# Row sums of the modulation sections by another route, a reciprocal root in two parts, and two moved steps on ScalarE

## The chip, the core and the metric

The kernel runs on one core of a Trainium2 chip. Its engines work side by side, each through its own queue in order: TensorE (PE, matrix products and transposes; the loading of its stationary operand is shown apart as PEld), VectorE (DVE), ScalarE (ACT), GpSimd (POOL, nearly unused here), and SyncE (SP), which issues the weight transfers. They meet through semaphores. The metric is the device time of one execution in microseconds (us), the median of the runs shown. Lower is better.

## What is computed

Two transformer stacks of two layers each, one after the other, on 256 tokens of width 1024 (batch 1, all float32). In the first stack the six vectors that modulate each layer (shift, scale and gate, for the mixer and for the feed-forward part) come from a conditioning vector `c` through a 1024 x 6144 matrix, so that there are twelve sections of 1024 numbers. Cut to what the change touches:

```
for i in range(DEPTH):                                  # 2 layers: differential attention, short convolution
    mod = (silu_c @ ada_w[i] + ada_b[i])[:, None, :]
    sh1, sc1, g1, sh2, sc2, g2 = jnp.split(mod, N_MOD, axis=-1)
    h = modulate(rmsnorm(x, norm1_g[i]), sh1, sc1)
    ...                                                 # y = mixer(h)
    x = x + g1 * y
    x = x + g2 * swiglu(modulate(rmsnorm(x, norm2_g[i]), sh2, sc2), ffn_w_in[i], ffn_w_out[i])
...
p = p[:, :, 0] - lam_full * p[:, :, 1]                  # differential attention, 8 heads of width 128
o = rmsnorm(o, subln_g) * (1.0 - lam_init)              # root mean square of each head of each token
y = o.reshape(B, n, D_MODEL) @ wo
...
b_gate, c_gate, u = jnp.split(t @ w_in, 3, axis=-1)     # short convolution
z = c_gate * u
conv = conv_w[0] * zp[:, 0:n] + conv_w[1] * zp[:, 1:1+n] + conv_w[2] * zp[:, 2:2+n]
y = (b_gate * conv) @ w_out
...
o = block_attention(q, k, v)                            # second stack, layer 2: 16 heads
y = (o.reshape(B, S, H * MLA_V) * jax.nn.silu(z)) @ w_out
```

## The kernel before

**Weights.** All weight matrices are cut into 147 units of up to 128 x 2048 numbers, loaded in order into a ring of three slots (`raw`). ScalarE makes the high part of a unit (`prepare`, line 585, a rounded copy), VectorE the low part (`split`, line 998, raw minus high), and TensorE multiplies three times: high with high, high with low, low with high. A full unit is 48 passes on TensorE. Unit u+3 goes into the slot of unit u; its high part waits for its load and for TensorE's end with unit u, and is made where an engine's queue says `behind(u)`. The stages are: start and keys, queries, values (`da_in`, `da_q`, `da_v`, 12 units), differential attention over 16 pairs of token block and head, its output (`da_out`, 4), a feed-forward part (`ffn0`, 33), the short convolution (`sc_in`, 12, and `sc_out`, 4), `ffn1` (33), and then the second stack, which ends with the attention of the layer MLA and its output.

**Modulation.** The first two sections are needed at the start: TensorE multiplies sixteen pieces of the matrix by the conditioning vectors, in four groups of 32 output rows at once (line 1811), and the four partial rows are summed with a matrix `sel2` (line 1828) which also turns them into columns. For the other ten VectorE scales and adds eight pieces of 128 x 1024 each into `ada_acc` (lines 975 and 977, `piece`), and then TensorE sums over the 128 partitions: eight products with `ada_acc` stationary and one column of ones moving (line 1648), whose result is already a column of 128 x 8 in PSUM bank 7. VectorE adds the bias in `section` (lines 988 to 991). These ten stand behind units 2 of `da_q`, 1 and 3 of `da_v`, 8, 14, 20 and 26 of `ffn0`, 2 and 11 of `sc_in`, and 5 of `ffn1`.

**End of the differential attention.** For each of 16 steps i, TensorE turns the probabilities (line 1636) and multiplies them by V (line 1916), VectorE scales the result into `XN` (line 1190), and ScalarE squares it and sums (`da_square`, line 691). Then VectorE takes the reciprocal root of all 16 sums (lines 1013 to 1035), scales the four groups of `XN` (line 1198), TensorE turns them (`output_groups`), ScalarE writes the high parts (line 606), VectorE the low parts (line 1045), and the first output unit starts once two low parts are there.

**Short convolution.** `sc_in` is four rounds of three units (c, u, b). VectorE takes out each product (`scaled`, line 1242, tiles tc, tu, tg), makes the low part of the unit three on, convolves (lines 1302 to 1304) and closes with line 1311. ScalarE copies tc into `cg` (line 746) and then makes the high parts of three units.

**Attention of MLA.** It goes by pairs of heads p = 0 to 7. VectorE finds the maxima (line 1410), ScalarE takes exponentials (`exps`, line 788) and copies turned probabilities (`turned`, line 910), VectorE scales the exponentials (line 1554) and for every second pair gates two banks of heads (line 1560), whose high part is made by ScalarE (`gated_high`, line 606) and whose low part by VectorE (`gated_low`, line 1565).

Every engine's order is the order in which the code is written; nothing reorders it.

## Time and profile before

| | us |
|---|---|
| runs before, median of 3 | 1090.65 (1090.09 to 1091.9) |
| the profiled execution, device time | 1092.87 |
| its span in the trace | 1090.8 |
| TensorE busy, share of the span | 95% |
| VectorE busy | 72% |
| ScalarE busy | 47% |
| mean granted TensorE clock | 0.982 |

The profile lists busy times by engine and the costliest groups of instructions, the chain of work that ended last, and instructions in order of time with the idle time ahead of each and what ended it. The granted clock of TensorE is 1.0 at 2.4 GHz and 0.5 at 1.2 GHz. The profiled execution is 2.2 us longer than the median of the runs.

### The profile page before, as it was taken

The numbers are of one execution on the slowest core, as the hardware profiler recorded it, in microseconds if no ns is written. First come the engines' busy times: TensorE is split into PE (matmuls) and PEld (weight loads), VectorE is DVE, ScalarE is ACT, GpSimd is POOL, SyncE is SP. The second block draws the span as 40 slices with busy tenths as digits, with TensorE's granted clock in tenths as the row PEclk, the third lists the DMA queues.
The fourth block names the chain that finished last, engine by engine and source line by source line (L and its number), as shares of the span: only waits on it lengthen the run. The fifth ranks groups of instructions, "written<-read, shape, count | busy, mean of one in ns | idle before, by whom it ended". The sixth has DMA issues, their size and how long they took to land.

```text
span 1090.8 us, 18302 instructions
## 1 busy us (share of the span) xinstructions
PE 1035.3 (95%) x7740; PEld 960.9 (88%) x7740; DVE 790.3 (72%) x1184; ACT 509.4 (47%) x732; POOL 0.7 (0%) x6
## 2 busy tenths in 40 slices
PE   4899999799999999998999999999999999999895
PEld 2689875699999999998999999999987998997684
DVE  3689759668787887887986646568746568896665
ACT  3623238454434344424343444445347665457562
POOL 0000000000000000000000000000000000000000
PEclk9899999899999999999999999999999999999898
DMA  9769541038998987566746676564754053543130
GB/s 367 273 214 330 187 174 39 2 104 291 318 302 293 316 284 245 189 226 233 248 155 209 208 242 213 175 191 129 232 182 162 2 184 119 185 138 150 37 119 38
DMA packets 118592, 210.14 MB, mean 193 GB/s; under 512 B 4250, under 2 KB 82288, under 8 KB 118512
## 3 DMA queue, kind: packets, MB, share of 16 engines
q1 hardware_dynamic: 117764, 206.81, 55.9%
q10 hardware_dynamic: 748, 2.18, 0.5%
q8 instruction: 61, 1.00, 0.4%
q14 instruction: 19, 0.16, 0.1%
HBM read 207.92 MB, written 1.05 MB: 192 GB/s over the span
## 4 chain that ended last, share of the span: by engine, by line
PE 79%; DVE 12%; ACT 3%; issue 2%; DMA 1%; SPq 1%; DVEq 0%; ACTq 0%
PE PS L1625 12%; PE PS L1626 12%; PE PS L1627 12%; PE PS L1710 8%; PE PS L1729 8%; PE PS L1711 8%; DVE low L998 3%; PE PS L1636 3%; PE PS L1748 2%; PE PS L1749 2%; PE PS L1753 2%; PE PS L1843 1%; PE PS L1844 1%; DMA ada_raw<-in_ada_w 1%; PE PS L1916 1%
## 5 line engine op out<-in xcount | busy, mean ns | idle before, releaser
L998 DVE TENSOR_TENSOR low<-raw,high 128x2048 fp32r<-128x2048 f32 (+2 forms) x147 | 328.1, 2233 | 153.5 <-ACT high L585 153.1
L585 ACT ACTIVATE high<-raw 128x2048 fp32r<-128x2048 f32 (+2 forms) x147 | 273.1, 1866 | 226.0 <-PE PS L1627 111.2
L1710 PE MATMUL PS<-hH,high 128*128 128x258 f32 x896 | 221.8, 284 | 4.6 <-ACT high L585 1.9
L1711 PE MATMUL PS<-hL,high 128*128 128x258 f32 x896 | 220.3, 283 | 0.0
L1710 PEld LDWEIGHTS PS<-hH,high 128*128 128x128 f32 x896 | 169.8, 189 | 6.5 <-issue 2.9
L1711 PEld LDWEIGHTS PS<-hL,high 128*128 128x128 f32 x896 | 168.7, 188 | 0.1
L1729 PE MATMUL PS<-hH,low 128*128 128x258 f32 x896 | 126.3, 283 | 0.3
L1729 PEld LDWEIGHTS PS<-hH,low 128*128 128x128 f32 x896 | 115.6, 189 | 1.3 <-DVE low L998 1.3
L1625 PE MATMUL PS<-gH,high 128*128 128x256 f32 x352 | 98.5, 280 | 0.0
L1626 PE MATMUL PS<-gL,high 128*128 128x256 f32 x352 | 98.4, 280 | 0.0
L1627 PE MATMUL PS<-gH,low 128*128 128x256 f32 x352 | 98.2, 279 | 0.0
L977 DVE SCALAR_TENSOR_TENSOR ada_acc<-ada_raw,cond,ada_acc 128x1024 f32<-128x1024 f32 x70 | 89.6, 1281 | 4.9 <-DMA ada_raw<-in_ada_w 2.6
L1625 PE MATMUL PS<-oH,high 128*128 128x256 f32 x256 | 74.7, 292 | 1.8 <-issue 1.8
L1627 PE MATMUL PS<-oH,low 128*128 128x256 f32 x256 | 74.1, 289 | 0.0
L1626 PE MATMUL PS<-oL,high 128*128 128x256 f32 x256 | 73.9, 289 | 0.0
L726 ACT ACTIVATE sil<-ta,shifts 128x256 f32<-128x256 f32 x44 | 20.0, 502 | 110.8 <-DVE ta L1242 110.8
L1625 PEld LDWEIGHTS PS<-gH,high 128*128 128x128 f32 x352 | 66.2, 188 | 0.2 <-DVE gL L1269 0.2
L1627 PEld LDWEIGHTS PS<-gH,low 128*128 128x128 f32 x352 | 66.0, 187 | 0.0
L1626 PEld LDWEIGHTS PS<-gL,high 128*128 128x128 f32 x352 | 66.0, 187 | 0.0
L1625 PEld LDWEIGHTS PS<-oH,high 128*128 128x128 f32 x256 | 50.4, 197 | 2.9 <-issue 2.6
L1626 PEld LDWEIGHTS PS<-oL,high 128*128 128x128 f32 x256 | 50.3, 196 | 0.0
L1627 PEld LDWEIGHTS PS<-oH,low 128*128 128x128 f32 x256 | 50.1, 196 | 0.0
(325 smaller groups left out, 1945.8 us busy)
## 6 DMA issues: line engine op xcount, KB each, us to landing
raw<-in_ffn_w_in SPq DMA_DIRECT2D x44, 1024.0 KB, 6.4
ada_raw<-in_ada_w SPq DMA_DIRECT2D x82, 512.0 KB, 5.4
raw<-in_ffn_w_out SPq DMA_DIRECT2D x22, 1024.0 KB, 6.0
raw<-in_na_w_in SPq DMA_DIRECT2D x16, 1024.0 KB, 5.5
raw<-in_da_wqkv SPq DMA_DIRECT2D x12, 1024.0 KB, 8.8
raw<-in_sc_w_in SPq DMA_DIRECT2D x12, 1024.0 KB, 5.7
raw<-in_ple_w_gate SPq DMA_DIRECT2D x8, 1024.0 KB, 4.8
raw<-in_mla_w_in SPq DMA_DIRECT2D x7, 1024.0 KB, 5.4
```

Source lines behind the costliest of these rows:

```text
L585: nc.scalar.activation(high[s][:, 0:width(u)], raw[s][:, 0:width(u)], ACT.Copy).then_inc(high_ready, 1)
L977: V_.scalar_tensor_tensor(acc[:, :], ada_raw[p % RING][:, :], cond[:, k, 0:1], acc[:, :], ALU.mult, ALU.add).then_inc(ada_used_dve, 1)
L998: V_.tensor_tensor(low[s][:, 0:w], raw[s][:, 0:w], high[s][:, 0:w].bitcast(F), ALU.subtract).then_inc(low_dve, 1)
L1625: MM(o, wH, xH, start=start, stop=False, skip_group_check=shared)
L1626: MM(o, wH, xL, start=False, stop=False, skip_group_check=shared)
L1627: return MM(o, wL, xH, start=False, stop=stop, skip_group_check=shared)
L1636: last = nc.tensor.transpose(PS[0:n, b, c:c + w], src, ident[0:w, 0:w])
L1710: MM(PS[:, b + c, 0:SEQ + 2], high[s][w(j, c)], hH[:, j, 0:SEQ + 2], start=j == 0, stop=False)
L1711: MM(PS[:, b + c, 0:SEQ + 2], high[s][w(j, c)], hL[:, j, 0:SEQ + 2], start=False, stop=False)
L1729: last = MM(PS[:, b + c, 0:SEQ + 2], low[s][w(j, c)], hH[:, j, 0:SEQ + 2], start=False, stop=j == KC - 1)
L1748: MM(o(c), high[s][w(j, c)], hH[:, j, 0:SEQ], start=j == 0 and c == 0, stop=False, skip_group_check=True)
L1749: MM(o(c), high[s][w(j, c)], hL[:, j, 0:SEQ], start=False, stop=False, skip_group_check=True)
```

## The change

1. The sum over partitions of a section (the ten later ones) is made by four products with 32 columns of ones stationary and 256 columns of `ada_acc` moving, each in its own group of 32 output rows of bank 7. ScalarE copies the 128 x 256 result to `sum_rows` (a tile that is free at the time), TensorE turns it by two transposes at a later place in its queue (bank 7, 6 or 5), and VectorE's `section` is split into a note (`section`) and the work (`section_turned`).
2. The first two sections: `sel2` is gone, eight transposes each take the place of eight products, and VectorE sums the four partial rows with one reduction.
3. At the end of the differential attention the root of the first 12 sums is spread over steps 13, 14 and 15, two groups are scaled inside step 15, the last four sums get a root of their own afterwards, and the fourth group is turned after the first output unit.
4. In `sc_in` ScalarE makes the first of a round's three high parts ahead of the copy to `cg`.
5. In the attention of MLA ScalarE makes `gated_high` ahead of the exponentials of the same step.

```diff
+def rows_bank(u, first):
+    if u < first["ffn0"]:
+        return 7
+    return 6 if first["sc_in"] <= u < first["ffn1"] else 5
...
+            def copy_rows(u):
+                if u in reduce_at:
+                    seen.next(rows_made)
+                    nc.scalar.activation(sum_rows[:, :], bank(7, SEQ), ACT.Copy).then_inc(rows_copied, 1)
...
             def ffn_phase(u0):
                 for i in range(FSTEPS):
                     ua = u0 + (3 * i - 1 if i else 0)
+                    copy_rows(ua)
                     seen.next(a_taken)
...
             for j in range(4):
                 u = first["sc_in"] + 3 * j
+                behind(u)
                 seen.next(c_taken)
                 for c in range(2):
                     ins = nc.scalar.activation(cg[:, c, :], tc[:, c, :], ACT.Identity, bias=shifts[:, c:c + 1])
                 ins.then_inc(c_copied, 1)
-                behind(u)
                 behind(u + 1)
                 behind(u + 2)
+                copy_rows(u + 2)
...
                 turned(2 * p + 1)
+                if p % 2 == 0 and p:
+                    gated_high(p // 2 - 1)
                 if p + 2 < 8:
                     exps(2 * p + 4, False)
                     exps(2 * p + 5, False)
-                if p % 2 == 0 and p:
-                    gated_high(p // 2 - 1)
...
-                src = PS[:, (7, 0)[g], 0:16].rearrange("p (c m) -> p m c", m=2)
+                four_rows = PS[:, 4 + 2 * g:6 + 2 * g, :].rearrange("p b (c j m) -> p (b c) m j", c=4, j=4)[:, :, 0:2, :]
+                src = (nwt, var)[g][:, 0:16].rearrange("p (c m) -> p c m", m=2)
+                link(V_.tensor_reduce(src, four_rows, AX.X, ALU.add))
...
+                if i == 13:
+                    v.wait_ge(sq_ready, 12)
+                    link(V_.tensor_scalar(var[:, 0:12], ssq[:, 0:12], 1.0 / P, EPS, ALU.mult, ALU.add))
+                    root_guess(var[:, 0:12], rst[:, 0:12], nwt[:, 0:12])
+                if i == 14:
+                    root_series(nwt[:, 0:12], poly[:, 0:12])
+                if i == 15:
+                    root_closed(rst[:, 0:12], nwt[:, 0:12], poly[:, 0:12])
+                    da_scaled(0, 0)
+                    da_scaled(1, 0)
                 seen.next(made_v)
...
+            da_scaled(0, 1)
+            da_low(0, 0)
+            da_low(1, 0)
             v.wait_ge(sq_ready, 16)
-            inverse_root(0, 16, P)
...
+            inverse_root(12, 16, P)
+            da_scaled(1, 1)
+            da_low(0, 1)
+            da_low(1, 1)
...
+            def turn_rows():
+                if not turning:
+                    return
+                b = rows_bank(turning.pop(), first)
+                seen.next(rows_copied)
+                claim(b)
+                transposes(b, [(h * P, P, sum_rows[:, h * P:(h + 1) * P]) for h in range(2)]).then_inc(section_made, 1)
+                owed(section_taken, b)
...
                 claim(7)
-                owed(section_taken, 7)
-                for c in range(KC):
-                    last = MM(PS[:, 7, c:c + 1], ada_acc[g % 2][:, c * P:(c + 1) * P], ones[:, 0:1], start=True, stop=True)
-                last.then_inc(section_made, 1)
+                for j in range(4):
+                    last = MM(PS[32 * j:32 * j + 32, 7, 0:SEQ], ones[:, 0:32], ada_acc[g % 2][:, j * SEQ:(j + 1) * SEQ],
+                              start=True, stop=True, tile_position=(0, 32 * j))
+                last.then_inc(rows_made, 1)
+                owed(rows_copied, 7)
+                turning.append(u)
...
-                for c in range(KC):
-                    if c == 4:
-                        pe.wait_ge(acc_half, g + 1)
-                    last = MM(PS[:, b, 2 * c:2 * c + 2], ada_acc[g][:, c * P:(c + 1) * P], sel2[:, :], start=True, stop=True)
+                for n in range(2):
+                    b = 4 + 2 * g + n
+                    pe.wait_ge((acc_copied, acc_half)[n], g + 1)
+                    claim(b)
+                    last = transposes(b, [(c * P, P, ada_acc[g][:, (4 * n + c) * P:(4 * n + c + 1) * P]) for c in range(4)])
...
-            output_groups(xn_ready, BY_HALF)
+            output_groups(xn_ready, BY_HALF[:3])
```

How the instructions stand on an engine, before and in the changed kernel (line numbers of each kernel). TensorE in `ffn0`, around the section behind unit 8. Before:

```order
L1729 MATMUL PS<-hH,low 128x258 x8
L1648 MATMUL PS<-ones,ada_acc 128x1 [waits g_ready,ada_used_dve]
L1648 MATMUL PS<-ones,ada_acc 128x1 x7
L1710 MATMUL PS<-hH,high 128x258 [waits g_ready,high_ready]
L1711 MATMUL PS<-hL,high 128x258
```

In the changed kernel, the products behind unit 8 and, one unit later, the two transposes:

```order
L1810 MATMUL PS<-hH,low 128x258 x8
L1725 MATMUL PS<-ada_acc,ones 32x256 [waits g_ready,ada_used_dve]
L1725 MATMUL PS<-ada_acc,ones 32x256 x3
L1791 MATMUL PS<-hH,high 128x258 [waits g_ready,high_ready]
L1792 MATMUL PS<-hL,high 128x258
...
L1810 MATMUL PS<-hH,low 128x258 x8
L1701 MATMUL PS<-ident,wide 128x128 [waits a_taken,rows_copied]
L1701 MATMUL PS<-ident,wide 128x128
L1690 MATMUL PS<-gH,high 128x256 [waits low_dve,hid_low]
```

Eight narrow products became four wide ones on 32 rows each and, behind the next unit, two transposes that wait for ScalarE's copy.

ScalarE at the start of `sc_in`, first round and the start of the second. Before:

```order
L585 ACTIVATE high<-raw 128x2048 [waits blocks_done,raw_in0]
L746 ACTIVATE cg<-tc,shifts 128x256 [waits c_taken]
L746 ACTIVATE cg<-tc,shifts 128x256
L585 ACTIVATE high<-raw 128x2048 [waits blocks_done,raw_in1]
L585 ACTIVATE high<-raw 128x2048 [waits blocks_done,raw_in2]
L585 ACTIVATE high<-raw 128x2048 [waits blocks_done,raw_in0]
L752 ACTIVATE oH<-cf 128x512 [waits conv_staged]
L746 ACTIVATE cg<-tc,shifts 128x256 [waits c_taken]
```

In the changed kernel:

```order
L594 ACTIVATE high<-raw 128x2048 [waits blocks_done,raw_in0]
L594 ACTIVATE high<-raw 128x2048 [waits blocks_done,raw_in1]
L765 ACTIVATE cg<-tc,shifts 128x256 [waits c_taken]
L765 ACTIVATE cg<-tc,shifts 128x256
L594 ACTIVATE high<-raw 128x2048 [waits blocks_done,raw_in2]
L594 ACTIVATE high<-raw 128x2048 [waits blocks_done,raw_in0]
L603 ACTIVATE wide<-PS 128x256 [waits rows_made]
L771 ACTIVATE oH<-cf 128x512 [waits conv_staged]
L594 ACTIVATE high<-raw 128x2048 [waits blocks_done,raw_in1]
L765 ACTIVATE cg<-tc,shifts 128x256 [waits c_taken]
```

One high part of each round now stands ahead of the wait for tc, and the copy of the row sums (tile `wide`) stands behind the other two.

VectorE in the last steps of the differential attention, steps 14 and 15 and the root. Before:

```order
L1174 SCALAR_TENSOR_TENSOR gates<-ada_raw,ratio 128x512 [waits dve_step]
L1190 TENSOR_SCALAR XN<-PS,rsum 128x128 [waits made_v] x2
L1013 TENSOR_SCALAR var<-ssq 128x16 [waits sq_ready]
L1022 TENSOR_SCALAR rst<-var 128x16 [waits dve_step]
L1028 TENSOR_TENSOR nwt<-rst 128x16 [waits dve_step]
```

In the changed kernel:

```order
L1219 SCALAR_TENSOR_TENSOR gates<-ada_raw,ratio 128x512 [waits dve_step]
L1062 TENSOR_SCALAR nwt<-nwt 128x12
L1063 TENSOR_SCALAR poly<-nwt 128x12 [waits dve_step]
L1064 TENSOR_TENSOR poly<-poly,nwt 128x12 [waits dve_step]
L1255 TENSOR_SCALAR XN<-PS,rsum 128x128 [waits made_v,dve_step]
L1069 SCALAR_TENSOR_TENSOR poly<-poly,nwt 128x12
L1069 SCALAR_TENSOR_TENSOR poly<-poly,nwt 128x12 [waits dve_step]
L1070 SCALAR_TENSOR_TENSOR rst<-poly,rst 128x12 [waits dve_step]
L1225 TENSOR_TENSOR XN<-XN,rst 128x512 [waits dve_step]
L1225 TENSOR_TENSOR XN<-XN,rst 128x512
L1255 TENSOR_SCALAR XN<-PS,rsum 128x128 [waits made_v]
L1225 TENSOR_TENSOR XN<-XN,rst 128x512
```

Ten root steps over 12 sums (four of them in step 13, ahead of these rows) and two scalings now stand ahead of VectorE's last line 1190 (now 1255).

## Rows read from the trace of the kernel before

**Rows 1.** Stretch of `ffn0`: us, busy time by engine, granted clock, DMA share, GB/s.
```profile
242.00:443.00 201.00, 199.32 (x1655) 197.75 (x1654) 164.76 (x175) 84.28 (x84) 0.00 (x0) 1.00 0.84 280
```

**Rows 2.** TensorE in order of time at a section in `ffn0`: start, us, instruction, count.
```profile
288.63 1.84 PE L1648 MATMUL PS<-ones,ada_acc 128*128 128x1 f32 x16
...
290.54 0.28 PE L1711 MATMUL PS<-hL,high 128*128 128x258 f32 x1
290.66 0.28 PE L1710 MATMUL PS<-hH,high 128*128 128x258 f32 x1
```

**Rows 3.** TensorE in order of time: row groups, then wide sums, then transposes.
```profile
30.07 0.62 PE L1811 MATMUL PS<-first_w,cond 128*32 128x512 f32 x2 [1.31 <-DMA ada_raw<-in_ada_w]
30.08 0.62 PE L1811 MATMUL PS<-ada_raw,cond 128*32 128x512 f32 x2
30.52 0.60 PE L1811 MATMUL PS<-first_w,cond 128*32 128x512 f32 x2
...
933.28 1.03 PE L1762 MATMUL PS<-XN,ones 128*128 128x256 f32 x4
...
26.80 1.97 PE L1636 MATMUL PS<-ident,XN 128*128 128x128 f32 x16
```

**Rows 4.** The start, in order of time: TensorE, ScalarE, TensorE.
```profile
31.92 1.28 PE L1828 MATMUL PS<-sel,ada_acc 128*128 128x2 f32 x10
...
33.49 1.91 ACT L585 ACTIVATE high<-raw 128x2048 fp32r<-128x2048 f32 x1 [0.83 <-DMA raw<-in_da_wqkv]
36.97 0.60 ACT L645 ACTIVATE dH<-da_V,mod_ctx 128x256 fp32r<-128x256 f32 x1 [1.57 <-DVE mod L1094]
...
39.01 0.77 PE L1843 MATMUL PS<-dH,high 128*128 128x512 f32 x1 [2.62 <-DVE dL L1111]
```

**Rows 5.** End of the differential attention, in order of time: VectorE, then TensorE.
```profile
204.07 0.35 DVE L1190 TENSOR_SCALAR XN<-PS,rsum 128x128 f32<-128x128 f32 x1 [1.93 <-PE PS L1916]
204.89 0.17 DVE L1013 TENSOR_SCALAR var<-ssq 128x16 f32<-128x16 f32 x1 [0.47 <-ACT rope_T L691]
206.99 2.50 DVE L1198 TENSOR_TENSOR XN<-XN,rst 128x512 f32<-128x512 f32 x4
...
207.74 3.67 PE L1636 MATMUL PS<-ident,XN 128*128 128x128 f32 x16 [3.70 <-DVE XN L1198]
211.27 0.58 PE L1625 MATMUL PS<-oH,high 128*128 128x256 f32 x1
```

**Rows 6.** `sc_in`, VectorE from the first to the fourth round; TensorE, start of `sc_out`.
```profile
450.48 0.68 DVE L1242 TENSOR_TENSOR tc<-PS,rstd 128x512 f32<-128x512 f32 x1
...
470.93 0.68 DVE L1242 TENSOR_TENSOR tc<-PS,rstd 128x512 f32<-128x512 f32 x1
474.39 2.29 DVE L998 TENSOR_TENSOR low<-raw,high 128x2048 fp32r<-128x2048 f32 x1 [2.78 <-ACT high L585]
...
511.14 0.68 DVE L1242 TENSOR_TENSOR tc<-PS,rstd 128x512 f32<-128x512 f32 x1
...
517.00 0.55 PE L1625 MATMUL PS<-oH,high 128*128 128x256 f32 x1 [1.79 <-issue]
```

**Rows 7.** Attention of MLA, in order of time: VectorE, then TensorE.
```profile
1017.83 0.69 DVE L1565 TENSOR_TENSOR oL<-X,oH 128x512 fp32r<-128x512 f32 x1 [1.92 <-ACT oH L606]
...
1023.57 1.08 PE L2206 MATMUL PS<-PT,V 128*64 128x256 f32 x8 [2.60 <-ACT PT L910]
```

**Rows 8.** Stretches, columns as in rows 1: at half clock, and one after.
```profile
39.00:45.00 6.00, 6.00 (x14) 4.74 (x15) 5.89 (x12) 6.00 (x11) 0.00 (x0) 0.50 0.13 40
207.00:212.00 5.00, 4.26 (x19) 4.01 (x20) 4.67 (x7) 2.61 (x4) 0.00 (x0) 0.50 0.00 0
212.00:215.00 3.00, 3.00 (x27) 3.00 (x25) 0.82 (x2) 0.14 (x1) 0.00 (x0) 0.96 0.03 5
517.00:523.00 6.00, 6.00 (x29) 6.00 (x30) 5.86 (x8) 1.17 (x1) 0.00 (x0) 0.51 0.76 262
1024.00:1029.00 5.00, 4.31 (x23) 2.48 (x18) 0.69 (x1) 3.02 (x4) 0.00 (x0) 0.56 0.00 0
```

More of the change, by code:

```diff
@@ L978, in piece, with section, section_turned @@
                                             ALU.mult, ALU.add).then_inc(ada_used_dve, 1)
-            def section(g):
+            turning = []
+            def section(u):
+                turning.append((reduce_at[u], rows_bank(u, first)))
+            def section_turned():
+                if not turning:
+                    return
+                g, b = turning.pop()
                 layer, part = divmod(g, 6)
@@ L1000, in sections @@
             def sections(u):
+                section_turned()
                 if u in reduce_at:
-                    section(reduce_at[u])
+                    section(u)
             def behind(u):
@@ L1182, in _ @@
             da_max(2)
+            section_turned()
             for i in range(16):
@@ L1637, in transposes @@
                 return last
+            turning = []
+            def turn_rows():
+                if not turning:
+                    return
+                b = rows_bank(turning.pop(), first)
[3 more added lines that the diff above has]
+                owed(section_taken, b)
             def behind(u):
+                turn_rows()
                 if u not in reduce_at:
```

62 lines of the change are left out of this document (39 added, 23 removed).

## The prediction

> **What bounds the kernel now.** The page says that TensorE is busy for 95% of the span, so I looked first for what fills it and then for the places where it waits. The table by stretches shows the feed-forward part full: 199.3 us busy out of 201, at full clock [rows 1]. What is taken off TensorE there comes off the time, and what is put beside it costs nothing as long as VectorE (165 us) and ScalarE (84 us) keep ahead. The chain of waits and TensorE's timeline then show four places where it isn't full: the start, where ScalarE waits for the modulation [rows 4]; the end of the differential attention, where the root stands between the last product and the output [rows 5]; the short convolution, where VectorE sets the pace [rows 6]; and the last pairs of MLA's attention [rows 7]. Each of the four has a stretch at half clock (1.2 GHz instead of 2.4) with it [rows 8]. The change touches all five places.
>
> **The ten later sections.** In one of them 16 passes (each product takes two) start at 288.63, one ordinary pass follows, and the next starts at 290.54. Ordinary passes come 0.12 apart (290.54 to 290.66), so the section holds TensorE for 290.54 - 288.63 - 0.12 = 1.79 us [rows 2]. In its place come four products in four row groups. Their form is there already: four passes of 512 columns start together (30.07, 30.08) and the next four 0.45 us later [rows 3], so with 256 columns a set of four takes 0.22, and the two sets 0.44. With about 0.1 for the first set's weights that is 0.55. The two transposes: 16 of them take 1.97 us from the first start to the last end, of which 0.27 is the tail of the last, so some 0.11 each [rows 3], and 0.25 for two. Together 0.80, saved 1.0 a section, 10 us for ten. From both sides: at the cheapest 0.44 + 0.22 = 0.66 (saved 1.1, 11 us); if the row groups didn't overlap, 8 passes at (1.03 - 0.38) / 3 = 0.22, the step within the wide sums [rows 3], are 1.76, with the transposes 2.0: a loss of 0.2 each. I take 1.0, since the row groups at 30.07 [rows 3] are the same form, with a stationary operand of 32 columns each. ScalarE's copy of 128 x 256 (estimated at 0.4, a fifth of its 1.91 for 128 x 2048 [rows 4] and a fixed part) and VectorE's later `section_turned` lie beside TensorE's next unit of 48 x 0.12 = 5.8 us. The queue to watch is TensorE's: the second bank of the next unit (bank 7) now waits for the copy, 2.9 us after the products, and the transposes wait for it too, 5.8 us after. In `ffn0` the copy stands ahead of the wait for ta, which nothing else holds up; behind it are silu and a high part, both with microseconds to spare. In the attention the copy delays one high part and one pair of exponentials by 0.4, which I count as nothing.
>
> **The start.** Two times 16 passes of line 1828 become two times 8 transposes; a reduction on VectorE (some 0.25, an estimate from the 0.17 of a short operation [rows 5]) is added behind each. Before, the passes ran from 31.92 and ScalarE began with dH at 36.97, having waited 1.57 for the modulation [rows 4]. Now the sixteen transposes take 16 x 0.11 from 31.92, to about 34.0, and VectorE's steps bring the modulation to about 34.9. Then ScalarE is late: its high part ends at 33.49 + 1.91 = 35.4, held by the load of its weights. So dH starts at 35.4 instead of 36.97, and TensorE at 37.45 instead of 39.01: 1.55 us earlier. It runs at half clock there, until about 45 [rows 8]. If the clock comes back at the same moment, only half of the gain stays: 0.8. If it comes back as long after the work became continuous as before, 1.55 stays. After the other stretches it came back sooner (4.5 us after the transposes began at 207.74, rows 5 and 8), which would make it 2.8. I take 2.0.
>
> **The root in two parts.** Step 15 has 1.93 us of idle time on VectorE ahead of 204.07 [rows 5]. A root step is (206.99 - 204.89) / 10 = 0.21, a scaling 2.50 / 4 = 0.63. Three root steps and two scalings, 1.9, fit exactly; for the four and three steps in 13 and 14 (0.8 and 0.6) I count a delay of 0.1, since those steps wait for products in the same way. So the first two groups are ready when the last product ends at 204.04, and TensorE turns them from 204.0 instead of 207.74. From the first transpose to the first output product it took 3.53 us [rows 5], now a little less since ScalarE and VectorE have both groups in hand: 207.3 instead of 211.27. Off this go 0.5 for the fourth group's transposes, which now stand between output units one and two, and are no part of the front any more. At full clock the gain would be 3.5, and 0.5 more since the half clock of the old start disappears. But half clock held from about 205 until 212.2 [rows 8], and the first output unit now runs inside it: at full length 4.9 / 2 = 2.45 lost, so 1.0 to 1.6 left. I take 2.2, range 1.0 to 4.1.
>
> **The short convolution.** In each round VectorE waits 2.78 us ahead of the first low part, because ScalarE first copies tc to cg and then makes the high part [rows 6]. From the first to the fourth round are 511.14 - 450.48 = 60.7 us; in it TensorE has nine units of 5.76, 51.8, and a section of 1.8, so it waits 7.0. Then it waits 1.79 more ahead of `sc_out` (517.00), and then runs at half clock for 5.8 us, 2.7 lost by the count of passes [rows 8]. With the high part ahead of the copy VectorE's round is 20.2 - 2.8 = 17.4 against 17.3 on TensorE: they are level, and what VectorE had as a lead at the first round (about 1.5 us) has to last. I followed each unit: the low part of the third unit of a round comes 1 to 2 us ahead of its use, and the banks are free in time. The high part itself needs a load that ended long before and the end of a unit that VectorE passed 7 us ago. So nearly all the waits go, the gap ahead of `sc_out` goes, and with it the half clock: 7.0 + 1.8 + 2.7 = 11.5, less 1 for waits that stay because the two engines are level, and 1 for the case that the clock still falls once: 9.5. From both sides: all of it, 11.5; or half the waits and the half clock remain, 4.
>
> **The attention of MLA.** VectorE waits 1.92 ahead of a low part whose high part stands behind four exponentials [rows 7], and with it the next pair's scaling and maxima come late; two steps on, TensorE waits 2.60. It happens at p = 2, 4 and 6, the last with nothing behind it. With the high part first VectorE doesn't wait, and TensorE's 2.60 shrinks by 1.9. Then there is the half clock from about 1024.6 to 1031.4, whose first 5 us show a clock of 0.56 [rows 8], and which costs 3.1 if the pass times are halved. It began in the wait of 2.60; with a shorter wait it may not. I take 2.5, from 1.6 to 4.6.
>
> **The sum.** 10.0 + 2.0 + 2.2 + 9.5 + 2.5 = 26.2. The profiled execution took 1092.87 (span 1090.8 and 2.07 around it), giving 1066.7; it lies 2.2 above the median of the runs, so 1064.5 for the median.
>
> **A rule weighed.** The sixteen transposes ran from 207.74 to 211.41 at half clock, and the clock was back at 212.2, less than 1 us after the products began [rows 5, 8]. The Trainium skill ("TensorE: Matmul & The Clock Gate", Part 4: PE-mode transpose) says that transposes don't count as TensorE activity in the way that products do. The trace speaks against it here, since such a quick return suggests that they did count. By the rule the transposes that now stand where products stood (the start) or where nothing stood (204.0 to 205.9) would not help the clock; this is the second rival.
>
> **Rivals.** (a) *VectorE still sets the pace of the convolution.* For it: 17.4 against 17.3 leaves nothing for a late load. Against it: DMA is busy for 0.76 of the time right behind it, less than the 0.84 of `ffn0` [rows 1, 8], where loads hold up nothing. Half the waits and the half clock remain: 4 instead of 9.5, so 1070. (b) *The half clock stays in all three short places,* at its full length or more. For it: in each there still is a gap of 1 to 3 us, and at the end of the attention the new work is in the stretch itself. Start 0.8, root 1.0, MLA 1.6, together 3.4 instead of 6.7: 1068. (c) *The row groups don't overlap,* sections lose 0.2 each: 26.2 - 12 = 14.2, so 1076.5; the starts at 30.07 and 30.52 speak against it [rows 3]. (d) *Slower: TensorE waits for ScalarE's copy.* The copy is in the queue behind high parts of 1.9 us and waits for products that TensorE has just made; each time it is late for bank 7, TensorE stands still in the middle of a unit, and the half clock can follow. The whole forecast gain is 26.2, so it decides from 2.6 us a section on, if it befalls all ten; at 3 us each the time would be 1064.5 + 30 = 1094.5. Against it: in `ffn0` ScalarE is busy for 84 of 201 us. (e) *The edits don't reach the path at all* (a load bounds each stage): within 0.2% of 1090.65. Only 13% of the DMA's time is used at the half-clock start, so I see nothing for it.
>
> **How the numbers follow.** Forecast 0.50, (b) 0.22, (a) 0.16, (c) 0.05, (d) 0.02, (e) 0.03, and 0.02 for more than all upper bounds. All upper bounds: 11 + 2.8 + 4.1 + 11.5 + 4.6 = 34, so 1056.7; all lower ones without (c): 9 + 0.8 + 1.0 + 4 + 1.6 = 16.4, so 1074.3. The range of 8 in 10 takes in the forecast's own spread, (b), and most of (a): 1059 to 1072. About 0.2% is what a measurement of this kernel can tell from no change: faster 0.95 (all but (d) and (e)), same 0.03, slower 0.02.
>
> **What would show it.** In the changed kernel's trace: a section on TensorE of 0.55 and 0.25 us instead of 1.79; sets of four passes 0.22 apart; VectorE without the 2.78 us ahead of the first low part of a round, and `sc_out` starting some 10 us sooner relative to `sc_in`; the last product of the differential attention and the first output product 3.3 us apart instead of 7.4; the wait of 2.60 below 1. It would be wrong if TensorE waited on ScalarE's copy (line 603 of the changed kernel) or if a granted clock of 0.5 stood in a stretch where it was 1.0.

## The result and the profile after

The changed kernel takes 1063.61 us (median of four runs, 1061.31 to 1064.19), the kernel before 1091.07 (four runs). The ratio is 0.9745 with a 95% interval of 0.9728 to 0.9762, a gain of 27.5 us. The forecast was 1064.5 in a range of 1059 to 1072. The total is right. Its terms are less so, and the rows and the experiments below tell them apart.

The page of the changed kernel begins so:

```profile
span 1061.4 us, 18186 instructions
...
PE 1013.9 (96%) x7664; PEld 936.2 (88%) x7664; DVE 791.2 (75%) x1195; ACT 512.2 (48%) x742; POOL 0.7 (0%) x6
```

The span is 29.4 us shorter (1090.8 - 1061.4). To see where, I subtracted the starts of the first pass of each of the 147 weight units in the two traces. The difference grows in steps, and only in these places:

| place | gain in the two profiled executions, us | forecast |
|---|---|---|
| start, up to the second unit of keys | 3.1 | 2.0 |
| each later section: 1.00 to 1.06 less in one unit, mostly 0.16 to 0.18 more in the next | 8.7 in ten | 10.0 |
| differential attention and its root (its section taken off) | 2.8 | 2.2 |
| short convolution up to the second unit of `sc_out` (its two sections taken off) | 9.8 | 9.5 |
| attention of MLA and first output unit | 4.8 | 2.5 |
| everything else together | 0.2 | 0 |

**A section.** TensorE in order of time in the changed kernel, in `ffn0`: ordinary passes, the products in row groups (L1725), ordinary passes, and one unit later the two transposes (L1701). It answers [rows 2].

```profile
279.29 1.12 PE L1810 MATMUL PS<-hH,low 128*128 128x258 f32 x8
280.35 0.64 PE L1725 MATMUL PS<-ada_acc,ones 128*32 128x256 f32 x8
280.91 0.39 PE L1791 MATMUL PS<-hH,high 128*128 128x258 f32 x1
281.14 0.29 PE L1792 MATMUL PS<-hL,high 128*128 128x258 f32 x1
281.26 0.28 PE L1791 MATMUL PS<-hH,high 128*128 128x258 f32 x1
...
286.80 0.38 PE L1701 MATMUL PS<-ident,wide 128*128 128x128 f32 x2
286.94 0.37 PE L1690 MATMUL PS<-gH,high 128*128 128x256 f32 x1
```

From the first product to the first ordinary pass are 0.56 us, as forecast (0.55). But the pass behind it is slow: the next one comes after 0.23 instead of 0.12. And the eight passes ahead take 280.35 - 279.29 = 1.06 instead of 0.96. By the same measure as in the prediction the products hold TensorE for 281.14 - 280.35 - 0.12 = 0.67 plus 0.10 ahead, 0.77 instead of 0.55. The transposes cost 0.16 to 0.18 by the unit starts and not 0.25. Net 1.04 - 0.17 = 0.87 a section.

**The short convolution.** VectorE: the starts of three rounds, and the first low part of the first and the second round. They answer [rows 6], where the low part stood 2.78 us of idle time behind the product.

```profile
438.49 0.68 DVE L1306 TENSOR_TENSOR tc<-PS,rstd 128x512 f32<-128x512 f32 x1
439.08 2.28 DVE L1029 TENSOR_TENSOR low<-raw,high 128x2048 fp32r<-128x2048 f32 x1
...
455.98 0.68 DVE L1306 TENSOR_TENSOR tc<-PS,rstd 128x512 f32<-128x512 f32 x1
...
456.65 2.28 DVE L1029 TENSOR_TENSOR low<-raw,high 128x2048 fp32r<-128x2048 f32 x1
...
473.56 0.68 DVE L1306 TENSOR_TENSOR tc<-PS,rstd 128x512 f32<-128x512 f32 x1
```

The idle time is gone, and rounds are 17.5 and 17.6 us apart (forecast 17.4). On TensorE a section and `sc_out` follow one another without a wait, where 1.79 us stood before:

```profile
495.30 0.64 PE L1725 MATMUL PS<-ada_acc,ones 128*32 128x256 f32 x8
495.87 0.39 PE L1690 MATMUL PS<-oH,high 128*128 128x256 f32 x1
```

**The end of the differential attention.** TensorE in order of time in the changed kernel: the last products, the transposes of three groups, the first output product. They answer [rows 5].

```profile
198.86 1.16 PE L1996 MATMUL PS<-da_V,gates 128*128 128x128 f32 x8 [0.69 <-ACT gates L701]
199.86 1.04 PE L1701 MATMUL PS<-ident,XN 128*128 128x128 f32 x8
201.06 0.66 PE L1701 MATMUL PS<-ident,XN 128*128 128x128 f32 x4 [0.17 <-DVE XN L1225]
202.92 0.39 PE L1690 MATMUL PS<-oH,high 128*128 128x256 f32 x1 [1.20 <-DVE oL L1088]
```

The wait of 3.70 us ahead of the transposes is gone. What is left is 1.20 us ahead of the output, in which TensorE waits for VectorE's low part.

**The attention of MLA.** VectorE's low part and TensorE's last wait in the changed kernel, which answer [rows 7]:

```profile
990.75 0.68 DVE L1630 TENSOR_TENSOR oL<-X,oH 128x512 fp32r<-128x512 f32 x1
...
997.20 1.08 PE L2289 MATMUL PS<-PT,V 128*64 128x256 f32 x8 [1.70 <-ACT PT L929]
```

VectorE's 1.92 is gone, but TensorE's 2.60 became 1.70, not "below 1". I had not looked for two earlier waits in the trace of before, 0.28 at 1010.16 and 0.70 at 1014.90, which are gone too. Together 0.28 + 0.70 + 0.90 = 1.9, the 1.9 of the forecast by another way.

**The granted clock.** Stretches of the changed kernel (us, busy time by engine, granted clock, DMA share, GB/s): start, start a little later, middle of the differential attention, its output, `sc_out`, end of MLA's attention. They answer [rows 8].

```profile
37.00:40.00 3.00, 2.78 (x7) 2.23 (x8) 2.93 (x8) 3.00 (x6) 0.00 (x0) 0.50 0.94 305
41.00:44.00 3.00, 3.00 (x15) 2.46 (x14) 3.00 (x5) 3.00 (x8) 0.00 (x0) 1.00 0.00 0
163.00:166.00 3.00, 3.00 (x9) 1.17 (x9) 2.36 (x6) 2.06 (x7) 0.00 (x0) 0.53 0.95 322
203.00:209.00 6.00, 6.00 (x51) 6.00 (x52) 2.81 (x11) 0.00 (x0) 0.00 (x0) 1.00 0.00 0
496.00:502.00 6.00, 6.00 (x51) 6.00 (x52) 5.75 (x9) 2.01 (x2) 0.00 (x0) 1.00 0.91 327
999.00:1003.00 4.00, 3.26 (x27) 2.50 (x26) 1.82 (x2) 3.89 (x5) 0.00 (x0) 1.00 0.02 4
```

Leaving out the tail of the kernel, half clock (1.2 GHz) held before from 34.73 to 44.97, 205.39 to 212.22, 516.01 to 522.83 and 1024.59 to 1031.42, 30.7 us. After, it holds from 36.87 to 40.28 and from 163.16 to 166.57, 6.8 us. The last three stretches of before are gone, and one in the attention is new. The change did nothing at 163: the same wait of 1.72 us stands ahead of it in both kernels.

### The profile page after: what moved, and what is told of

The parts are those of the page before. It is cut to its first block, busy times and chain, and to the rows that moved or that the text cites. A ratio compares the mean times of both kernels' runs of the same rounds, so it can differ in the third digit from the quotient of the medians.

```text
span 1061.4 us, 18186 instructions
## 1 busy us (share of the span) xinstructions
PE 1013.9 (96%) x7664; PEld 936.2 (88%) x7664; DVE 791.2 (75%) x1195; ACT 512.2 (48%) x742; POOL 0.7 (0%) x6
## 3 DMA queue, kind: packets, MB, share of 16 engines
HBM read 207.92 MB, written 1.05 MB: 197 GB/s over the span
## 4 chain that ended last, share of the span: by engine, by line
PE 84%; DVE 9%; ACT 2%; DMA 2%; issue 1%; SPq 1%; DVEq 0%; ACTq 0%
PE PS L1690 12%; PE PS L1691 12%; PE PS L1692 12%; PE PS L1791 9%; PE PS L1792 9%; PE PS L1810 9%; PE PS L1701 3%; DVE low L1029 2%; PE PS L1829 2%; PE PS L1830 2%; PE PS L1834 2%; DMA raw<-in_da_wqkv 2%; PE PS L1996 1%; PE PS L1922 1%; PE PS L1923 1%
## 5 line engine op out<-in xcount | busy, mean ns | idle before, releaser
L1690 PEld LDWEIGHTS PS<-oH,high 128*128 128x128 f32 x256 | 48.2, 188 | 2.2 <-DVE oL L1088 1.4
```

Of the source, the lines that this page charges most:

```text
L1690: MM(o, wH, xH, start=start, stop=False, skip_group_check=shared)
```

## The experiments

### Each part undone

Five kernels are the changed one with one part put back. First u_conv, ScalarE's order in `sc_in`:

```diff
-                behind(u)
                 seen.next(c_taken)
...
                 ins.then_inc(c_copied, 1)
+                behind(u)
                 behind(u + 1)
```

> The changed kernel with ScalarE's order in sc_in put back (copy to cg ahead of the first high part of a round). Theory: the order alone makes the 10 us between the first and the last unit of the short convolution, waits on VectorE of 2.8 us a round come back, TensorE waits 1.8 ahead of sc_out and the half clock after it comes back: 1063.6 + 10 = 1073.6. Rival: part of the gain in this stretch comes from the two shorter sections inside it (their 0.8 each gives VectorE a lead), and the clock falls less often in any case: then only 4 to 7 us come back, and no stretch at half clock stands at the start of sc_out.

u_mla, ScalarE's order in the attention of MLA:

```diff
-                if p % 2 == 0 and p:
-                    gated_high(p // 2 - 1)
                 if p + 2 < 8:
                     exps(2 * p + 4, False)
                     exps(2 * p + 5, False)
+                if p % 2 == 0 and p:
+                    gated_high(p // 2 - 1)
```

> The changed kernel with gated_high put back behind the exponentials in the attention of MLA. Theory: the wait of 2.6 on TensorE comes back and the half clock at the end of the attention with it, 4.9 us in all (3.7 up to the first unit of mla_out, 1.1 behind it): 1068.5. Rival: the half clock there depends on what stood before (it fell from a different moment), then only the wait itself, 1.9 to 2.6, comes back and the clock stays full: 1066.

u_root, the root in one piece and all four groups turned ahead of the output:

```diff
-                if i == 13:
...
-            inverse_root(12, 16, P)
+            inverse_root(0, 16, P)
...
-            output_groups(xn_ready, BY_HALF[:3])
+            output_groups(xn_ready, BY_HALF)
```

> The changed kernel with the root of all 16 sums in one piece behind the last product, and the fourth group turned ahead of the output. Theory: last product to first output product goes from about 3.1 back to 7.4 us, a half clock from about 199 on returns with it, and the one near 163 is not touched, so 4.5 to 5.5 us come back: 1068.5. Rival: the stretch at half clock near 163 (new in the changed kernel, where the kernel before had it at 205) has the same origin and there is one or the other; then the one at 163 goes when this one comes, and the net is 2.8 us, the step read from the two traces: 1066.4.

u_sections, the ten later sections as before:

```diff
-                for j in range(4):
-                    last = MM(PS[32 * j:32 * j + 32, 7, 0:SEQ], ones[:, 0:32], ada_acc[g % 2][:, j * SEQ:(j + 1) * SEQ],
-                              start=True, stop=True, tile_position=(0, 32 * j))
...
+                for c in range(KC):
+                    last = MM(PS[:, 7, c:c + 1], ada_acc[g % 2][:, c * P:(c + 1) * P], ones[:, 0:1], start=True, stop=True)
...
```

ScalarE's copy and the two transposes are gone in it too.

> The changed kernel with the ten later sections summed as before (eight narrow products each, no copy on ScalarE, no transposes). Theory: each costs 0.85 us more, as the steps between units in ffn0 show (1.0 less for the unit with the products, 0.15 more for the one with the transposes), 8.5 in all: 1072.1. Rival: the sections also bought VectorE a lead in the short convolution and the differential attention, and the stretch at half clock near 163 comes from the wait behind the shorter section; then it is 10 to 12 with changed waits in sc_in, or 7 with the half clock at 163 gone.

u_start, the first two sections as before:

```diff
-                for n in range(2):
...
-                    last = transposes(b, [(c * P, P, ada_acc[g][:, (4 * n + c) * P:(4 * n + c + 1) * P]) for c in range(4)])
+                for c in range(KC):
...
+                    last = MM(PS[:, b, 2 * c:2 * c + 2], ada_acc[g][:, c * P:(c + 1) * P], sel2[:, :], start=True, stop=True)
```

> The changed kernel with the first two sections made as before (sixteen passes against sel2 each, no reduction on VectorE). Theory: dH starts 1.8 us later on ScalarE, and the half clock lasts from about 35 to 45 again as in the kernel before: 3.1 us come back, 1066.7. Rival: the length of the stretch at half clock varies by itself and has nothing to do with the sixteen transposes; then 1.8 come back and the stretch ends about 3.4 us after it began: 1065.4.

What they took:

| kernel | median, us | ratio to before | above 1063.61 | forecast of the term |
|---|---|---|---|---|
| u_conv | 1074.78 | 0.9848 (0.9831 to 0.9864) | 11.2 | 9.5 |
| u_mla | 1067.60 | 0.9788 (0.9773 to 0.9803) | 4.0 | 2.5 |
| u_root | 1067.08 | 0.9783 (0.9768 to 0.9797) | 3.5 | 2.2 |
| u_sections | 1071.56 | 0.9822 (0.9807 to 0.9836) | 8.0 | 10.0 |
| u_start | 1064.48 | 0.9746 (0.9722 to 0.9771) | 0.9 | 2.0 |

The five add up to 27.6, the whole gain is 27.5: beyond the spread of the runs the parts are not seen to help or hinder one another. An interval of these ratios is 3 to 5 us wide, so a single term is known to some 2 us, and the start can't be told from nothing by its time.

u_conv decides for the order of ScalarE's work as the cause. Only the order was put back, and both signs are there, VectorE's idle time ahead of the low part and TensorE's wait and half clock at `sc_out`. VectorE and TensorE in order of time in u_conv, then one of its stretches:

```profile
462.73 2.29 DVE L1029 TENSOR_TENSOR low<-raw,high 128x2048 fp32r<-128x2048 f32 x1 [2.71 <-ACT high L594]
...
505.34 0.36 PE L1690 MATMUL PS<-oH,high 128*128 128x256 f32 x1 [2.90 <-issue]
```
```profile
506.00:509.00 3.00, 3.00 (x16) 3.00 (x15) 2.93 (x5) 0.91 (x2) 0.00 (x0) 0.50 0.91 288
```

In u_mla the wait of 2.60 is back, and half clock holds from 999.92 to 1003.33. TensorE in order of time:

```profile
991.24 1.08 PE L2289 MATMUL PS<-PT,V 128*64 128x256 f32 x8 [0.71 <-ACT PT L929]
...
999.92 1.98 PE L2289 MATMUL PS<-PT,V 128*64 128x256 f32 x8 [2.60 <-ACT PT L929]
1001.83 1.81 PE L1701 MATMUL PS<-ident,E 128*128 128x128 f32 x8
```

Eight passes take 1.98 there and 1.08 in the changed kernel. Over the attention this trace is 3.6 us longer. Waits explain 0.29 + 0.71 + 2.60 - 1.70 = 1.9 of it, the clock the other 1.7. The rival, only the wait, falls for this profile, and the kernel before shows the same pair, a wait of 2.60 and half clock behind it.

u_root lies between its theory and its rival. Its stretch from 201.48 to 208.31 is the one of before, and none stands near 163 in it. So at first it looked as if there was one or the other; the repeat of the changed kernel below takes that back.

u_sections shows steps of 1.03 to 1.05 us in the units with products and of -0.15 to -0.17 in the next ones, 0.87 each. There is no half clock near 163 in it either.

u_start has its first product at 38.55 instead of 37.22. Yet its half clock holds from 34.61 to 41.44, and not to 45 as in the kernel before. Neither of the two ends that I had set is met.

### The four row groups, one behind the other

```diff
-                    last = MM(PS[32 * j:32 * j + 32, 7, 0:SEQ], ones[:, 0:32], ada_acc[g % 2][:, j * SEQ:(j + 1) * SEQ],
-                              start=True, stop=True, tile_position=(0, 32 * j))
+                    last = MM(PS[:, 7, 0:SEQ], ones[:, :], ada_acc[g % 2][:, j * SEQ:(j + 1) * SEQ],
+                              start=j == 0, stop=j == 3)
```

> The changed kernel with the four products of each later section on all 128 output rows, one behind the other, instead of in four row groups (the row sums are then wrong in value, since all four pieces are added up). Theory: side by side the eight passes take 0.55 us, one behind the other 8 x 0.22 = 1.76 or more exactly 8 x 0.12 = 0.96, as other passes of 256 columns start 0.12 apart at full clock: by the second figure the section grows by 0.4, so 1063.6 + 4 = 1067.6; by the first, the price I used for the rival in the prediction, by 1.2: 1075.6.

It took 1073.28 us, ratio 0.9826 (0.9801 to 0.9852), 9.7 above the changed kernel. TensorE in order of time at the first section of `ffn0`:

```profile
282.07 1.89 PE L1725 MATMUL PS<-ada_acc,ones 128*128 128x256 f32 x8
283.61 0.47 PE L1791 MATMUL PS<-hH,high 128*128 128x258 f32 x1
283.91 0.28 PE L1792 MATMUL PS<-hL,high 128*128 128x258 f32 x1
```

By the measure of the prediction the eight passes hold TensorE for 283.91 - 282.07 - 0.12 = 1.72 instead of 0.77. They start (1.89 - 0.38) / 7 = 0.22 apart, and not 0.12 (0.38 is the last one's own length). In four groups they cost less than half. Between the traces each section costs 1.0 more (10.2 in ten, with the lengths of the half clock at the start and near 163 allowed for), while the eight narrow products of before cost 0.87 more (u_sections). Done one behind the other the new form would have lost some 0.15 a section against the old one, close to my price for that rival, 0.2. The medians say the same, 1073.28 against 1071.56 of u_sections, though their intervals overlap.

The edit changes a second thing: the stationary operand has 128 columns of ones instead of 32. That this narrower operand is what saves the time was not tested by itself, but the rows of the changed kernel speak against it. There the second set of four starts 0.24 after the first (280.35 and 280.59). So a set of four takes what one pass takes here (0.22). The narrower passes are no faster; they run four at a time.

### ScalarE's copy a little later

```diff
-                    copy_rows(ua)
                     seen.next(a_taken)
                     ...
                     ins.then_inc(silu_ready, 1)
+                    copy_rows(ua)
```

> The changed kernel with ScalarE's copy of the row sums behind silu instead of ahead of the wait for ta, in the two feed-forward parts (five sections; the others unchanged). It prices the rival in which TensorE waits for the copy: silu ends 285.9 in the trace, the copy 286.3, TensorE reaches bank 7 at about 283.9, so it waits 2.4 us in each of five sections: 12 us, 1075.6, and up to 2.5 us each more if the clock falls in the wait: 1088 at most. Rival: the queue has enough slack that the wait is hidden by later waits of the unit; 1064.

It took 1068.33 us (1064.84 to 1069.03), ratio 0.9775 (0.9746 to 0.9805), 4.7 above. The interval touches that of the changed kernel, and one of the four runs took no longer than it, so the reading rests on the trace. Of the five sections one shows a step: the unit behind the first section of `ffn0` has TensorE waiting in its middle, and half clock from 288.51 to 291.92 behind that. ScalarE, TensorE and a stretch of p_late_copy:

```profile
286.49 0.91 ACT L743 ACTIVATE sil<-ta,shifts 128x256 f32<-128x256 f32 x2 [5.09 <-DVE ta L1306]
287.31 0.36 ACT L603 ACTIVATE wide<-PS 128x256 f32<-128x256 f32 x1
```
```profile
287.72 0.39 PE L1791 MATMUL PS<-hH,high 128*128 128x258 f32 x1 [2.12 <-ACT wide L603]
```
```profile
289.00:292.00 3.00, 3.00 (x16) 3.00 (x16) 2.50 (x2) 0.47 (x1) 0.00 (x0) 0.51 1.03 406
```

The 2.12 and half of the 3.4 us at half clock make the 3.9 us of the step. At the other four sections VectorE takes out `ta` as soon as TensorE is done (it waited for that 0.30 us, until 321.18, one section on), the copy is in time, and nothing is lost. So the slower rival of the prediction is real as a mechanism, but far off: in the changed kernel ScalarE's copy ends at 281.05 + 0.39 = 281.44, and TensorE's first pass that needs the bank starts at 283.92. ScalarE has to be 2.5 us later than it is to meet the rival, and even with a copy later than that it came in one place in five. My figure of 12 us took one row for all five.

### VectorE's low part out of the attention

```diff
-                if i == 0:
-                    split(first["da_v"] + 3 + RING)
...
             da_low(1, 1)
+            split(first["da_v"] + 3 + RING)
```

> The changed kernel with VectorE's low part of the unit da_out+2 taken out of the first step of the differential attention and put behind the last low part at its end. Theory: VectorE has no idle time in steps 1 to 12, so its 2.3 us are on the path; TensorE's wait of 1.72 at 161 goes, and the half clock that followed it (163.16 to 166.57, 1.7 us of passes at half pace) with it: 2 to 4 us less, 1060.5. Rival: TensorE or ScalarE sets the pace there, and the 1.72 come back elsewhere in the attention, or the half clock moves to a later wait: within 0.5 us of 1063.6.

It took 1060.90 us, ratio 0.9712 (0.9682 to 0.9742), 2.7 less than the changed kernel. The two intervals overlap, so the traces have to carry the reading. TensorE's wait of 1.72 in the first steps is gone, as these rows of n_split_late show (four transposes follow eight passes without idle time), and the clock is 1.00 from 163 to 166:

```profile
161.87 1.16 PE L1995 MATMUL PS<-da_V,gates 128*128 128x128 f32 x8
162.87 0.60 PE L1700 MATMUL PS<-ident,gates 128*128 128x128 f32 x4
```
```profile
163.00:166.00 3.00, 3.00 (x23) 1.91 (x21) 2.93 (x6) 2.38 (x9) 0.00 (x0) 1.00 0.00 0
```

The step over the attention is 3.5 us in the trace, 1.7 of the wait and 1.7 of the clock. The same trace had a longer half clock at its start (36.72 to 43.54) and lost 1.3 of this there. Only the wait is sure to be saved: a second profile of the changed kernel, further down, has full clock at this place with the wait still in it.

### What lets the clock fall: the wait filled

Two kernels are u_root with 26 passes put into its wait of 3.70 us, once as 13 products and once as 26 transposes of the same tile; nothing uses their results.

```diff
+            claim(0)
+            for k in range(13):
+                MM(bank(0, P), V[:, 0, 0:P], ident[:, :], start=True, stop=True)
             output_groups(xn_ready, BY_HALF)
```

The second has these lines in the place of the loop:

```diff
+            for k in range(26):
+                transposes(0, [(0, P, V[:, 0, 0:P])])
```

> u_root (the root in one piece, 3.7 us in which TensorE waits, half clock from 201.48 to 208.31) with 13 products of a tile of V with the identity, 26 passes of 128 columns into a bank that is free, put into that wait; their results are used by nothing. Theory: the clock falls because TensorE stands still ahead of the transposes; with 3.4 us of products in the wait no stretch at half clock begins there, and the output starts at the same time with its first 12 transposes and units at full pace: 1.9 + 0.6 us less than u_root's 1067.1, so 1064.6. Rival: the clock falls at that point for what went before, or the dense transposes behind the wait are themselves what lets it fall; then half clock stands at about 201 to 208 in this run too, and the time is 1067.

> u_root with 26 transposes of the same tile in the place of the 26 passes of products. If transposes keep the clock as products do, this run is like t_fill_products: 1064.6 and no stretch at half clock at about 201. If they don't count, as the page of the Trainium skill that the prediction weighs says, the clock falls here as in u_root or sooner: 1067 to 1068.

u_root's wait and a stretch:

```profile
202.56 3.67 PE L1689 MATMUL PS<-ident,XN 128*128 128x128 f32 x16 [3.70 <-DVE XN L1225]
```
```profile
202.00:207.00 5.00, 4.44 (x20) 4.18 (x21) 4.57 (x8) 2.75 (x4) 0.00 (x0) 0.50 0.00 0
```

TensorE in order of time and a stretch, first of t_fill_products:

```profile
202.15 3.07 PE L1989 MATMUL PS<-ident,da_V 128*128 128x128 f32 x26
206.01 2.46 PE L1689 MATMUL PS<-ident,XN 128*128 128x128 f32 x16 [0.80 <-DVE XN L1225]
```
```profile
206.00:209.00 3.00, 2.46 (x16) 1.67 (x16) 3.00 (x5) 2.29 (x4) 0.00 (x0) 1.00 0.00 0
```
And of t_fill_transposes:

```profile
199.91 3.00 PE L1689 MATMUL PS<-ident,da_V 128*128 128x128 f32 x26
203.76 2.46 PE L1689 MATMUL PS<-ident,XN 128*128 128x128 f32 x16 [0.85 <-DVE XN L1225]
```
```profile
203.00:206.00 3.00, 2.24 (x16) 1.67 (x16) 2.98 (x5) 1.54 (x3) 0.00 (x0) 1.00 0.00 0
```

In both, half clock is gone from this place, and the sixteen transposes take 2.46 instead of 3.67. So the two profiles with the wait of 3.70 (before and u_root) have half clock here, and the two with the wait filled do not: the wait was what let the clock fall, and the 26 transposes kept it up as the products did. That is one profile for each filling. The mean clock of all four executions of each kernel points the same way, 0.990 to 0.993 for u_root, 0.992 to 0.995 with the products and 0.993 to 0.994 with the transposes. The Trainium skill ("TensorE: Matmul & The Clock Gate", Part 4: PE-mode transpose) says that transposes don't count as activity in the same way; t_fill_transposes, with 1.00 from 200 on, doesn't agree with it.

The times don't show it: 1067.55 (0.9786, 0.9772 to 0.9799) and 1067.44 (0.9782, 0.9769 to 0.9796) against 1067.08 of u_root. From the second unit of keys to the second of the output both are 1.4 us shorter than u_root, once the half clock near 166 that t_fill_products had in its profile is allowed for, and not the 2.5 that I had expected, since the first output product waits for VectorE's low part at either clock (0.67 of idle time now stand ahead of it). The rest is hidden by the start, where the half clock was longer in both profiles (36.6 to 43.4, u_root 37.64 to 41.05). That the medians differ by less than that is within their spread; a gain in time wasn't shown for these two.

### The wait at the start filled, and the changed kernel once more

n_start_fill is n_split_late with one more edit:

```diff
                 last.then_inc(section_made, 1)
                 owed(section_taken, b - 1, b)
+            claim(0)
+            for k in range(11):
+                MM(bank(0, P), ones[:, :], ident[:, :], start=True, stop=True)
```

> n_split_late (1060.9) with 11 products of ones with the identity, 22 passes whose results are used by nothing, in the wait of TensorE at the start (33.9 to 37.2), behind the sixteen transposes. Theory: the half clock of 3.4 to 6.8 us that begins at about 36.7 comes from that wait; with the wait filled it doesn't begin, and da_in starts at the same time at full pace: 1.7 to 3.4 less, 1058.4. Rival: it comes from the sparse stretch before 30 and begins in any case, only sooner: 1060.9 or, if the first products of da_in have to wait for the fill at half clock, up to 1.5 more, 1062.4.

> The changed kernel as it is, on the same chip as the three others, to tell how far its times spread and to have a direct comparison. Theory: the start is the same code in every run, but the stretch at half clock there is 3.4 us long in some and 6.8 in others, and the one near 163 is there or not; so the times of one kernel spread over 1061.3 to 1064.5 with a median of 1063.5. Rival: the profiled execution's 3.4 us are the rule for this kernel; then the times lie within 1 us of one another.

n_start_fill took 1059.21 us (1058.84 to 1060.00), ratio 0.9708 (0.9695 to 0.9721). The changed kernel took 1064.17 (1062.25 to 1065.08) on the same chip, ratio 0.9755 (0.9741 to 0.9768). The two intervals lie apart: the two edits bring 5.0 us on top of the change. What the filling brings by itself the times don't tell: n_start_fill is 1.7 us below n_split_late, with intervals that overlap (0.9695 to 0.9721 and 0.9682 to 0.9742). Between the traces, up to the second unit of keys, it is 1.6 us against the repeated changed kernel (3.4 us of half clock there) and 3.0 against n_split_late (6.8 us). Stretches at the start, first of n_start_fill, then of the repeated changed kernel:

```profile
34.00:37.00 3.00, 2.46 (x22) 2.26 (x21) 1.79 (x8) 3.00 (x5) 0.00 (x0) 1.00 1.05 384
37.00:40.00 3.00, 2.51 (x11) 2.13 (x12) 2.93 (x7) 3.00 (x7) 0.00 (x0) 1.00 0.97 316
40.00:43.00 3.00, 3.00 (x15) 2.49 (x14) 2.96 (x7) 3.00 (x5) 0.00 (x0) 1.00 0.04 12
```
```profile
34.00:37.00 3.00, 0.00 (x0) 0.00 (x0) 1.73 (x8) 3.00 (x5) 0.00 (x0) 1.00 1.05 384
37.00:40.00 3.00, 2.53 (x9) 2.06 (x10) 2.93 (x8) 3.00 (x7) 0.00 (x0) 0.79 1.00 326
40.00:43.00 3.00, 3.00 (x10) 2.38 (x9) 2.96 (x7) 3.00 (x5) 0.00 (x0) 0.64 0.03 11
163.00:166.00 3.00, 2.63 (x16) 1.71 (x17) 2.93 (x7) 1.86 (x6) 0.00 (x0) 1.00 0.88 280
```

With the wait filled no half clock begins at the start. The last row is the second finding: the same code has no half clock near 163 here, where the first profile of it had 0.53. Twelve profiles have the wait of 1.72 ahead of that place. Half clock followed it in six (the first of the changed kernel, u_conv, u_mla, u_start, p_late_copy, t_fill_products) and not in six (the kernel before, u_root, u_sections, p_serial, t_fill_transposes, the repeat). So what I had read from u_root, one stretch or the other, was chance. At the start, too, eleven profiles share the changed kernel's code. Half clock came in all of them, held for 3.4 us in six and for 6.8 in five, and began anywhere from 35.9 to 38.8. The theory on the spread holds: nine runs of the changed kernel lie between 1061.31 and 1065.08.

## Why the prediction was right, point by point

- **Sections: right in kind, mis-sized.** Forecast 10.0 with bounds of 9 and 11, measured 8.7 by the unit starts and 8.0 by u_sections. The term that failed is the "0.1 for the first set's weights": entering and leaving the row groups costs TensorE 0.10 ahead and 0.11 behind, so 0.77 instead of 0.55, while the transposes were 0.08 cheaper. The step "the row groups overlap" was right, and p_serial shows that the whole gain of the sections hangs on it.
- **The start: right on what is late next, wrong on the clock.** dH started at 35.21 (forecast 35.4) and TensorE at 37.22 (37.45), 1.79 earlier. The two executions differ by 3.1, above my upper bound of 2.8, because the half clock was 3.4 us long in the one and 10.2 in the other. I took such a length for a property of the kernel, to be worked out from what precedes. Eleven profiles of the same code show two lengths. The bound of 2.8 does not come out of its own rows either: with half clock for 4.5 us instead of 5.96 it comes to 1.55 + (5.96 - 4.5) / 2 = 2.3. By u_start's time the edit brings 0.9, which its interval doesn't tell from nothing.
- **The root: right on the wait, wrong on the clock, in the other direction.** From the end of the last product (198.86 + 1.16 = 200.02) to the first output product (202.92) are now 2.9 us instead of 211.27 - 204.04 = 7.2 (the prediction's last paragraph has 7.4), a little better than forecast (3.3). I took 2.45 off because the output would begin inside a stretch at half clock. It does not: with the wait of 3.70 gone the clock doesn't fall (203 to 209 at 1.00), so the step "half clock held from about 205, and the first output unit now runs inside it" failed. That is 4.3 us; the 2.8 of the two traces has the half clock near 163 against it, which is there or not from one execution to the next. u_root says 3.5.
- **The convolution: right.** 9.5 forecast, 9.8 by unit starts, 11.2 by u_conv. All three parts (waits, the gap ahead of `sc_out`, the half clock) went, and the 2 us I had held back for two level engines and a clock that may still fall were not needed in this trace.
- **MLA: too small.** 2.5 forecast (1.6 to 4.6), 4.8 by unit starts, 4.0 by u_mla. The waits gave 1.9, as forecast, though spread over three places. The failed step is "it may not": I priced the end of the half clock at 0.6, and it went altogether, worth 1.7 in u_mla and 2.9 (4.8 - 1.9) against the longer stretch of before. TensorE still waits 1.70, and the clock stayed.
- **The rivals.** (a) did not come, (b) did not: half clock went in two of its three places and lasted less long in the third. (c) is refuted by the rows, and p_serial shows its price to have been about right, a loss of some 0.15 a section for my 0.2. (d) is priced by p_late_copy: 3.9 us in one of five places, and only with ScalarE more than 2.5 us later. (e) falls.

That the total came out within 1 us is luck: errors of both signs met, by the undone parts 2.0 too much on the sections and 1.1 on the start, 1.7 too little on the convolution, 1.5 on MLA and 1.3 on the root.

## What to carry to other kernels

Where an engine has work whose inputs came long ago (here a high part) in a queue behind something that waits, ask who waits for that work on the next engine: moving one call up was worth 11 us in `sc_in` and 4 in MLA, together nearly twice the new form of ten reductions. Count a wait of TensorE twice, for itself and for the half clock that can follow it, and where such a wait can't be removed, products of no use put into it can keep the clock, as the start shows; what they bring in time was small here and not told apart from the spread. Before a step of 1 to 3 us is given a cause, look for it in a second profile of the same code.

## What the runs showed of the hardware

- Four products on 32 output rows each share TensorE's time: eight passes of 256 columns hold it for 0.77 us (0.56 from the first to the next ordinary pass, 0.10 lost ahead and 0.11 behind), against 1.72 one behind the other on 128 rows each.
- Half clock began behind some waits and not behind others of the same length: behind the 1.72 us in the differential attention in six profiles of twelve, behind the 1.70 at the end of MLA's attention in none of the twelve profiles that have it, behind 2.60 in its place in both that have that. What decides was not settled.
- In a wait of 3.70 us 26 transposes (3.0 us of work) kept the clock at 1.00 as 26 passes of products did.
